# Block 0's weights in two transfers, C and B behind block 2's weights, block 1's low product last, and one softmax scaling a step earlier: a two-layer encoder trunk in float32

## What is computed

```python
for l in range(2):
    mod = silu(c) @ w_mod[l] + b_mod[l]
    sh1, sc1, g1, sh2, sc2, g2 = split(mod, 6)
    h = rmsnorm(x, norm1_g[l]) * (1 + sc1) + sh1
    q, k, v, ca, cb, su, gates = split(h @ w_in[l])
    y_attn = window_attention(rope(q), rope(k), v, sinks[l]) @ w_attn_o[l]
    y_conv = silu(layernorm(depthwise31(ca * sigmoid(cb)))) @ conv_pw_w[l]
    y_ssm  = glu(complex_scan(su; A, dt, B, C) + d * su)
    mixed  = gate_a * y_attn + gate_c * y_conv + gate_s * y_ssm
    x = x + g1 * (mixed @ w_out[l])
    h2 = rmsnorm(x, norm2_g[l]) * (1 + sc2) + sh2
    x = x + g2 * ((silu(h2 @ w_gate[l]) * (h2 @ w_up[l])) @ w_ffn_out[l])
return rmsnorm(x, final_norm_g)
```

## Time and profile before

| | |
|---|---|
| median of 3 runs | 933.24 us (932.68 to 933.51) |
| profiled execution: its time, its span | 935.88 us, 934.1 us |
| TensorE busy (matmul) | 905.1 us, 97% |
| TensorE busy (weight load) | 763.9 us, 82% |
| VectorE busy | 708.7 us, 76% |
| ScalarE busy | 486.4 us, 52% |
| GpSimd busy | 12.8 us, 1% |
| mean granted TensorE clock | 0.996 |
| moved by DMA | 196.10 MB, mean 210 GB/s |

### The profile page before, as it was taken

One profiled execution on the slowest core, in us unless ns is written; L12 is line 12 of the kernel. 1 busy time (PEld: TensorE's weight loads), 2 busy tenths in 40 slices (PEclk: granted clock), 3 DMA queues, 4 the chain that ended last, 5 costly groups with the idle time before them and its releaser, 6 DMA issues.

```text
span 934.1 us, 15663 instructions
## 1 busy us (share of the span) xinstructions
PE 905.1 (97%) x6575; PEld 763.9 (82%) x6575; DVE 708.7 (76%) x941; ACT 486.4 (52%) x606; POOL 12.8 (1%) x13
## 2 busy tenths in 40 slices
PE   5999999999999999999999999999999999999996
PEld 1898977777778999899988998777777888888885
DVE  3896898998677688676677689998957766666666
ACT  4794248743737674655345316883373643343334
POOL 2000000000000000000000000000000000000001
PEclk9999999999999999999999999999999999999999
DMA  8993366657896559847977534445778455555531
GB/s 355 241 275 122 134 223 226 232 203 280 303 262 222 176 177 334 315 141 241 311 258 166 156 133 136 140 149 196 257 296 293 157 194 190 181 180 192 195 109 46
DMA packets 128566, 196.10 MB, mean 210 GB/s; under 512 B 30730, under 2 KB 90642, under 8 KB 122352
## 3 DMA queue, kind: packets, MB, share of 16 engines
q1 hardware_dynamic: 126119, 194.89, 62.2%
q10 hardware_dynamic: 2376, 0.21, 0.2%
HBM read 194.02 MB, written 1.06 MB: 209 GB/s over the span
## 4 chain that ended last, share of the span: by engine, by line
PE 81%; DVE 8%; SPq 3%; DMA 3%; ACT 3%; issue 2%; ACTq 0%; DVEq 0%
PE bank L617 19%; PE bank L619 18%; PE bank L618 18%; PE bank L983 8%; PE bank L984 4%; PE bank L655 3%; DVE wlo L1570 2%; PE bank L721 2%; DVE yc L1880 1%; SPq L591 1%; DMA raw<-in_w_in 1%; DMA raw<-in_w_mod 1%; PE bank L745 1%; PE bank L733 1%; PE bank L903 1%
## 5 line engine op out<-in xcount | busy, mean ns | idle before, releaser
L1570 DVE TENSOR_TENSOR wlo<-raw,whi 128x2048 fp32r<-128x2048 f32 (+1 forms) x136 | 302.6, 2227 | 145.3 <-PE bank L619 73.2
L1176 ACT ACTIVATE whi<-raw 128x2048 fp32r<-128x2048 f32 x133 | 251.3, 1896 | 102.0 <-DMA raw<-in_w_in 51.4
L617 PE MATMUL bank<-hb,whi 128*128 128x256 f32 x592 | 170.4, 288 | 1.1 <-DVE wlo L1570 1.1
L619 PE MATMUL bank<-hb,wlo 128*128 128x256 f32 x592 | 167.6, 283 | 0.0
L618 PE MATMUL bank<-hb,whi 128*128 128x256 f32 x592 | 167.5, 283 | 0.0
L617 PE MATMUL bank<-whi,bhi 128*128 128x512 f32 x304 | 121.2, 399 | 0.3 <-DVE blo L1987 0.3
L983 PE MATMUL bank<-hb,whi 128*128 128x512 f32 x336 | 119.0, 399 | 0.0
L619 PE MATMUL bank<-whi,blo 128*128 128x512 f32 x304 | 118.8, 391 | 0.0
L618 PE MATMUL bank<-wlo,bhi 128*128 128x512 f32 x304 | 118.6, 390 | 0.0
L617 PEld LDWEIGHTS bank<-hb,whi 128*128 128x128 f32 x592 | 113.4, 192 | 3.9 <-DVE wlo L1570 1.7
L618 PEld LDWEIGHTS bank<-hb,whi 128*128 128x128 f32 x592 | 113.5, 192 | 0.4
(11 more groups left out here) (277 smaller groups left out, 1126.3 us busy)
## 6 DMA issues: line engine op xcount, KB each, us to landing
raw<-in_w_mod SPq DMA_DIRECT2D x48, 1024.0 KB, 5.5
raw<-in_w_ffn_in SPq DMA_DIRECT2D x44, 1024.0 KB, 5.1
raw<-in_w_in SPq DMA_DIRECT2D x38, 1024.0 KB, 7.2
raw<-in_w_ffn_out SPq DMA_DIRECT2D x22, 1024.0 KB, 5.0
raw<-in_w_out SPq DMA_DIRECT2D x8, 1024.0 KB, 7.5
raw<-in_w_in SPq DMA_DIRECT2D x16, 256.0 KB, 4.6
raw<-in_ssm_glu_b SPq DMA_DIRECT2D x4, 1024.0 KB, 6.3
raw<-in_ssm_glu_a SPq DMA_DIRECT2D x4, 1024.0 KB, 5.2
```

The source lines that it names most:

```text
L617: mm(o, w_hi, a_hi, start=start, stop=False, skip_group_check=True)
L619: return mm(o, w_lo, a_hi, start=False, stop=stop, skip_group_check=True)
L1176: fn(whi[mi % N_HI][:, n], raw[SLOT[item]][:, n], ACT.Copy).then_inc(hi_half if half == 0 else s_hi, 1)
L1570: part = V.tensor_tensor(wlo[mi % N_LO][:, n], raw[SLOT[("main", *divmod(mi, NB))]][:, n], whi[mi % N_HI][:, n].bitcast(F32), ALU.subtract)
```

## The change

What it does:

1. SP's queue begins with the modulation weights. c, ident and consts are issued by ScalarE, ahead of its own small vectors.
2. Block 0's weights come in two transfers of half a block with a semaphore each; ScalarE copies and TensorE uses them by halves.
3. On SP's queue C and the first part of B stand behind block 2's weights, with the late constants and the taps, ahead of block 3's.
4. On TensorE block 1 does its products with the high weights first, then C rounds 0 and 1, then those with the low weights. The C rounds leave block 0.
5. ScalarE doubles C and copies rounds 0 and 1 at block 1, ahead of `hi(3)`; it spreads B's first part at the end of block 1 instead of block 0. VectorE's two `b_source` move behind the `lo` of blocks 2 and 3.
6. Ten fillers of seventeen go.
7. In both layers `softmax_scale` of `r` = 3 stands ahead of `hi` of block 18.

```diff
-B_SPREAD_AT = [{0: 0, 2: 1}, {PREP_AT + 6: 1}]
+B_SPREAD_AT = [{1: 0, 2: 1}, {PREP_AT + 6: 1}]
...
-            sp.dma_start(crow[:, :], A["c"].rearrange("b (r c) -> (b r) c", c=P)).then_inc(s_c, 16)
-            sp.dma_start(ident[:, :], A["c_ident"]).then_inc(s_const, 16)
-            sp.dma_start(consts[:, :], A["c_small"]).then_inc(s_const, 16)
...
-                if item == ("main", 0, 2):
+                if item == ("main", 0, 3):
                     load_c(sp, 0)
                     load_b(sp, 0, 0)
-                if item == ("main", 0, 3):
                     late_constants(sp)
                     load_taps(sp, 0)
...
-                    for d, src in main(item[1], item[2], dst):
-                        sp.dma_start(d, src).then_inc(landed, 16)
+                    if item == ("main", 0, 0):
+                        ((d, src),) = main(0, 0, dst)
+                        sp.dma_start(d[:, 0:4], src[:, 0:4]).then_inc(s_first, 16)
+                        sp.dma_start(d[:, 4:8], src[:, 4:8]).then_inc(landed, 16)
+                    else:
+                        for d, src in main(item[1], item[2], dst):
+                            sp.dma_start(d, src).then_inc(landed, 16)
...
+                        if mi == 0 and k == 4:
+                            pe.wait_ge(s_hi, 1)
...
-                        for r in range(2):
-                            prep_round(0, r)
...
+                elif mi == 1:
+                    o = unit_bank(l, i)
+                    for k in range(DK):
+                        for c in range(2):
+                            for a in (hhi, hlo):
+                                mm(o[:, c * T:(c + 1) * T], w8[0][:, k, c * P:(c + 1) * P], a[:, k, :], start=(k == 0 and c == 0 and a is hhi), stop=False,
+                                   skip_group_check=True)
+                    for r in range(2):
+                        prep_round(0, r)
+                    middle()
+                    pe.wait_ge(s_lo[lo_engine(i)], LO_NO[(l, i)] + 1)
+                    for k in range(DK):
+                        for c in range(2):
+                            last = mm(o[:, c * T:(c + 1) * T], w8[1][:, k, c * P:(c + 1) * P], hhi[:, k, :], start=False, stop=(k == DK - 1),
+                                      skip_group_check=True)
+                    last.then_inc(s_unit, 1)
...
-            keep_busy(bank[0], 17)
+            keep_busy(bank[0], 7)
...
-                if t - 2 in SCORES_AT:
+                if t - 2 in SCORES_AT and SCORES_AT[t - 2] < 3:
                     softmax_scale(l, SCORES_AT[t - 2])
...
-            hi(0)
-            norm_hi(0, 0, DK)
+            hi(0, 0)
+            norm_hi(0, 0, 2)
+            hi(0, 1)
+            norm_hi(0, 2, DK)
             hi(1)
...
+                    if (l, i) == (0, 1):
+                        act.wait_ge(s_cc[0], 32)
+                        fn(once[:, :, 1, :], once[:, :, 0, :], ACT.Copy).then_inc(c_twice, 1)
+                        for n in range(2):
+                            round_copy(0, n)
...
+                    if SCORES_AT.get(2 * i - 1) == 3:
+                        softmax_scale(l, 3)
                     if i < NB - 1:
                         hi(l * NB + i + AHEAD)
...
-            b_source(0, 0)
...
-                    if (l, i) == (0, 0):
-                        b_source(0, 1)
+                    if l == 0 and i < 2:
+                        b_source(0, i)
```

More of the change, by code:

```diff
@@ L400, in trunk @@
         hi_half = sem("hi_half_ready")
+        s_first = sem("first_half_landed")
         s_lo = {"pool": sem("lo_ready_pool"), "dve": sem("lo_ready_dve")}
@@ L885, in main_block @@
                 W, V = whi[mi % N_HI], wlo[mi % N_LO]
-                if mi:
+                if mi == 1:
+                    pe.wait_ge(s_hi, 2)
+                elif mi:
                     pe.wait_ge(s_lo[lo_engine(i)], LO_NO[(l, i)] + 1)
                 else:
-                    pe.wait_ge(s_hi, 1)
+                    pe.wait_ge(hi_half, 1)
                 w8 = [w[:, :].rearrange("p (k n) -> p k n", k=DK) for w in (W, V)]
@@ L1171, in hi @@
                 item = ("main", *divmod(mi, NB))
-                act.wait_ge(s_land[SLOT[item]], LANDED[item])
+                if mi == 0 and half == 0:
+                    act.wait_ge(s_first, 16)
+                else:
+                    act.wait_ge(s_land[SLOT[item]], LANDED[item])
                 if mi >= N_HI:
@@ L1465, in side @@
                     taps_copy(l + 1)
+            act.dma_start(crow[:, :], A["c"].rearrange("b (r c) -> (b r) c", c=P)).then_inc(s_c, 16)
+            act.dma_start(ident[:, :], A["c_ident"]).then_inc(s_const, 16)
+            act.dma_start(consts[:, :], A["c_small"]).then_inc(s_const, 16)
             small_vectors(act, 0)
@@ L1480, in _ @@
             load_b(act, 0, 1)
-            hi(0)
-            norm_hi(0, 0, DK)
+            hi(0, 0)
+            norm_hi(0, 0, 2)
+            hi(0, 1)
+            norm_hi(0, 2, DK)
             hi(1)
-            act.wait_ge(s_cc[0], 32)
-            fn(once[:, :, 1, :], once[:, :, 0, :], ACT.Copy).then_inc(c_twice, 1)
-            for n in range(2):
-                round_copy(0, n)
             for l in range(DEPTH):
@@ L1563, in lo @@
                 if half == 0 and mi == NB + 1:
-                    dve.wait_ge(hi_half, 1)
+                    dve.wait_ge(hi_half, 2)
                 else:
```

## The result

The changed kernel takes 938.54 us (median of 4 runs, 938.45 to 939.96), the kernel before beside it 933.38 (932.68 to 933.68). The ratio is 1.0053, 95% interval 1.0041 to 1.0065: slower by 5.2 us, where 932.3 was forecast and the range ended at 935.2.

What follows compares the result with a forecast made beforehand. TensorE, busy 905.1 of 934.1 us, was taken as the bound, so only its waits or slower running count. Start +2.7 and layer 1 -3.6 gave -0.9, on the median 932.3 us; range 929.2 to 935.2.

Steps and rivals of the forecast that it cites:

- The start: Stretch to about 61 us: later B rounds +1.1 and half clock behind the new wait +1.6, together +2.7 us.
- Layer 1: Wait for the fourth set of probabilities at 627 us: moved scaling saves 1.8 wait and 1.8 half clock, -3.6 us.
- I take this 1.8 as gained too: Layer 1, behind the 1.9 us wait: half clock vanishes with the wait, saving another 1.8 us.
- they land at 48.7: At the start: the fourth block's weights (block 3) land at 48.7 us, bounds 46.5 and 51.9.
- The mechanism: At the start: B rounds wait for ScalarE's spread behind the fourth block's copy, starting 5.0 us after its weights land.
- The head start: SP's queue: first modulation block issued at 0.72 instead of 2.06, bringing the whole weight stream 1.3 us earlier.
- The small issues: SP's queue ahead of block 3's weights: five small issues partly run under B, so block 3's first issue comes at 41.8.
- The slower rival: At ScalarE's `hi(3)`: late fourth-block weights cost a microsecond each, outweighing layer 1 from 51.5; at 52.0 +2.4, 935.6; chance 0.08.
- Between them TensorE is full: TensorE between the start and the layer-1 wait: no slack, so a shift of the start is carried to the end.
- The clock at the start: Behind the 5.1 us wait ahead of the B rounds: half clock follows, +1.6 us, bounds 0 and +3.4.
- Block 0 starts earlier: TensorE at the start: with block 0's weights in halves it begins at 30.4 instead of 34.27 us.
- The moved scaling: Layer 1: scaling runs from 626.19 to 627.45, cutting TensorE's wait from 1.87 to about 0.1, a gain of 1.8 us.

Runs made afterwards that it cites:

- e2: Kernel before with only the fourth softmax scaling moved ahead of the weights' copy of block 18: 931.58 us, ratio 0.9974.
- e1: Kernel before, unchanged, run and traced a second time: 933.40 us, ratio 0.9996.
- e8: Changed kernel with the late constants and taps on SP's queue behind the fourth block's weights instead of ahead: 935.98 us, ratio 1.0022.
- e10: Changed kernel with C and B ahead of block 2's weights on SP's queue again, nothing else: 936.47 us, ratio 1.0022.
- e5: Changed kernel with c, ident and consts at the head of SP's queue again, as before: 938.00 us, ratio 1.0045.
- e12: Kernel before with 7 filler products in the layer-1 wait ahead of the transposes of the fourth set of probabilities: 933.84 us, ratio 0.9997.
- e6: Changed kernel with 44 filler products in the wait ahead of B rounds 2 and 3, which they overran: 938.30 us, ratio 1.0042.
- e9: Changed kernel with 22 filler products in the wait ahead of B rounds 2 and 3: 936.86 us, ratio 1.0029.
- e7: Kernel before with only block 0's weights in two transfers and ten fillers fewer: 935.17 us, ratio 1.0013.
- e4: Changed kernel with ScalarE's first spread of B ahead of its copy of the fourth block's weights again: 936.16 us, ratio 1.0022.
- e11: Changed kernel with e5's and e8's edits, both B spreads ahead of the weights' copies, and VectorE's second B source earlier: 932.61 us, ratio 0.9975.
- e3: The whole change without the moved softmax scaling, against the kernel before: 942.71 us, ratio 1.0093.

## Why the prediction was wrong

**The miss in the terms of the sum.** -0.9 was forecast and +5.2 measured, 6.1 apart. The start stood in the sum at +2.7. e2 and the changed kernel differ by the start alone, 931.58 and 938.54, so it cost 7.0 (7.4 by the ratios). Layer 1 stood in it at -3.6; e2 is 1.8 below the 933.38 of before in the result, and 2.2 below the runs beside it.

**The first step that failed: "I take this 1.8 as gained too" in layer 1.** The half clock behind the 1.9 us wait was priced rightly, 1.8 forecast and 1.6 measured (e1), but I read it from one execution and put it on the median. The text said that this execution was 2.6 above the median and carried the difference along as a constant. A good part of it was the very thing being removed: e1 shows the same wait without half clock, and e2 gives 2.2 for the move, where 3.6 was forecast. On the traced execution the layer-1 term is right: the transposes of the third set stood 5.97 later than before (614.04 to 620.01), the products with V of the fourth 2.62 later (634.24 to 636.86), a gain of 3.35.

**The second, and the larger: when the fourth block's weights land, "they land at 48.7".** It was 51.37, inside the bounds given (46.5 to 51.9) and near the bad end. The mechanism held: rounds 4.97 behind the landing in after and in e8; in e10 5.04 behind the start of the copy. Two inputs were off:

- *The head start, "-1.3".* It was a gain in issue time that reached no landing. consts, on ScalarE's queue, came at 9.26 instead of 3.60, so the first modulation product ran 2.6 later and the second at 15.18 instead of 12.47. The stream needs the buffers that these free: from 18 to 20 us it moved 283 GB/s, where before it moved 434. The last modulation product came 0.5 later, and block 2's weights at 40.91 instead of the 39.0 forecast. e5, which has neither the head start nor the late constants, has them at 40.90: the two together gave nothing, and what the head start alone would give no run shows. The prediction had looked for a cover on ScalarE's x, and not at who else waits for consts. The Trainium skill, DMA: Bandwidth & Descriptors, section "Issuing engines are not separate DMA queues", says that several issuers save only the time of issuing; e5 agrees, with no more than 0.2 us at the fourth block either way.
- *The small issues, "partly run under B".* The queue took 4.9 us for them (39.45 to 44.39). I had 41.8 for the issue behind them. e8 takes them away and has the weights 2.9 earlier.

At the changed kernel's own landing, my sum would have read: rounds at 56.4, the start 2.7 higher, +5.4. The modulation product behind block 5 came 5.3 later than in the traced execution of before (75.14), but 5.7, 5.8 and 6.4 later than in e12, e1 and e2 (74.76, 74.65, 74.08), which run the same code up to there. The fourth block's weights landed at 50.91 in the first and at 49.4 to 50.2 in the others, so the execution of before that I read had the latest start of four, and the agreement of 5.4 with 5.3 is in part luck. With the landing alone put right, the sum would have given +1.8, 935.0, still in the range; layer 1 adds 1.8, and 1.6 stands in no term.

The slower rival had the right place, and its chance of 0.08 rested on the wide bound being unlikely. Its point was wrong: by the sum's own terms (+2.7 at 48.7 and a microsecond for each one later) the start outweighs a layer 1 of 3.6 from 49.6 on; 51.5 is where the change is slower by 0.2%. With layer 1 at 2.2, the change breaks even at 48.2 and is slower by over 0.2% from 50.1 on.

**A premise that failed in part: "Between them TensorE is full".** From the modulation product behind block 5 to the third set of layer 1 the four traces with the old start take 538.9 to 539.2 us and the changed kernel 539.6. An idle stretch of 0.3 to 0.8 us that the profile doesn't name stands between 516 and 530 us in eight of the ten traces with block 0 in halves, and in none of the other four. The two without it are those with the fillers, e6 and e9, and e6 takes 537.4 us for the stretch. That it belongs to the change is likely by this count; its cause is open.

**What held.** The clock at the start: half clock was forecast at 1.6 and is 1.8 (e9), 1.7 of it at the end. The rule of the Trainium skill, TensorE: Matmul & The Clock Gate, section "HAM oscillation", that a DMA wait between bursts puts the array back to half rate, agrees with the traced waits of 2.5 us and more, which were for ScalarE; at 1.8 to 1.9 us one trace agrees and three do not. The Trainium skill, same page, Part 1, says of the rise of the clock under sustained work that its point varies from run to run; here the fall varies too, behind the same wait at the same place, and I had not reckoned with that. Block 0 starts earlier, if at 32.27 and not 30.4: the norm's first high part came at 31.61, since the modulation's end had moved by +0.5 and not by -1.3. The moved scaling removes its wait whole (e2).

**Where the expected gain of the start went.** Block 0's 2 us are lost at block 2, whose low part is late (e7, wait of 0.64 and what else was in step). The queue's new order brings block 2's weights 3.4 us earlier (40.91 against 44.34) and so TensorE to the rounds at 50.2; there it waits for the spread. With the spread put right (e4) the wait moves behind the second spread, 3.07; with that put right too (e11) a wait of 1.1 for a low part is the longest there, and rounds 6 and 7 stand where they stood, 59.78 against 59.86 in e1. That the weights' rate then sets this point, and no order can beat it, is argued only: no run changed the bytes.

**Sum.** From e1's trace to that of after: +5.8 at the modulation product behind block 5, +6.2 at layer 1's third set (613.80 to 620.01), and +4.5 at the end (932.2 to 936.7), 1.8 less. e1's traced execution is 0.7 above its median, after's is its median: 5.2, as measured. From e2's trace: +6.4, +7.1 (612.95 to 620.01) and +7.0 at the end (929.7 to 936.7), as the medians have it. So the start costs 6.4 of the 7.0 by 80 us, and 0.4 to 0.7 arise in mid-kernel.

## What to carry to other kernels

If the traced execution is slower than the median, find out what it holds more before a term is read from it; a clock drop or a stall that sits in one execution of several is not a saving for the median. When a step that waits for a late transfer stands in an in-order list, everything behind it inherits the landing: put ahead what is already ready. And an earlier first issue is no gain in itself: 1.35 us of it, with the small constants that the first consumer needs moved to another queue, left nothing at the fourth block. Last, microseconds of executions at the same mean clock compare better than ratios to a median that mixes two clocks.

## What the runs showed that was not expected

- The wait of 1.8 to 1.9 us ahead of the fourth set of probabilities is in four traces, and half clock followed in one (before), not in e1, e3 and e7. Behind the first 34 us, half clock followed waits of 2.53, 3.07, 3.16, 5.9, 6.03 and 6.15 us each time, and none of 1.65, 1.45, 1.37 (e12) and 1.22. It also followed an idle stretch of 0.83 in the midst of 64-column products (e3), but not one of the same length in e11 (522.47).
- At the start of the modulation stream eight products took 1.93 us (7.66) at a recorded clock of 1.00, the same eight took 1.06 later (24.91), in both kernels: in the first 20 us the recorded clock doesn't tell their speed.
- Part of the half clock can fall into the wait that precedes work (0.71 and 0.86 are the clocks from 50 to 55 us in e5 and after): e5's rounds 4 and 5 came 0.57 earlier than the changed kernel's relative to their landing, with the same wait (6.03 and 6.15).
- The four transfers of the fourth block landed 7.0 us behind their first issue in the changed kernel and 8.5 behind it in e8, where they follow B's at once: an issue moved ahead by 4.4 us brought 2.9.
- In 13 of 14 traces TensorE sits idle for 0.6 to 1.2 us between 85 and 94 us with no releaser named; only e6, where the start was latest, lacks it and makes up 1.4 us by 95 us.
